# The first input projection of the second block: its second weight chunk is requested at the landing of another gather

## The reference

```
u_sel = u[ids]                                  # 128 rows of 1024 per token
h     = gelu(einsum('td,ted->te', x, u_sel))    # one dot product per pick
v_sel = v[ids]
out   = einsum('te,ted->td', gates * h, v_sel)  # weighted sum of 128 rows
x     = layer_norm(alpha * x + out)
```

## Time and profile before

| what | us |
|---|---|
| median of 3 runs | 2751.7 |
| lowest and highest | 2751.35, 2753.34 |
| span of the profiled execution | 2749.7 |
| TensorE busy in the span | 2495.3 |
| last gather used by VectorE (from the span's start) | 1558.26 |
| last mix of the expert stage ends | 1562.63 |
| chunk 1 and chunk 2 used up by TensorE | 1578.16 |

### The profile page before, as it was taken

The page is one execution under the profiler, slowest core; times in us unless marked ns, Lnnn a source line. Parts: engine busy times, 40 slices in busy tenths (PEclk is TensorE's granted clock), DMA queues, the critical chain, the costliest instruction groups (busy, mean ns, idle before and its releaser), DMA issues.

```text
span 2749.7 us, 29400 instructions
## 1 busy us (share of the span) xinstructions
PE 2495.3 (91%) x9829; PEld 1558.5 (57%) x9829; DVE 1761.0 (64%) x3952; ACT 995.1 (36%) x2016; POOL 652.1 (24%) x636
## 2 busy tenths in 40 slices
PE   8989888798987999877877899999999999999999
PEld 4544443364452565533323357885688668865787
DVE  2678876766758667678776566554666556546654
ACT  2136322234322354223222145432444444424443
POOL 0134344433434324334444220002000020002000
PEclk9999999999999999999999999999999999999999
DMA  7599999999999999999999833543254415523452
GB/s 294 210 379 420 414 421 404 421 421 421 407 420 421 420 394 411 420 422 419 421 419 418 347 123 138 184 167 153 70 206 153 170 46 199 185 117 123 153 190 100
DMA packets 112402, 798.99 MB, mean 291 GB/s; under 512 B 13076, under 2 KB 15719, under 8 KB 20247
## 3 DMA queue, kind: packets, MB, share of 16 engines
q0 software_dynamic: 74464, 540.07, 47.7%
q1 hardware_dynamic: 37814, 257.40, 24.7%
HBM read 796.36 MB, written 4.22 MB: 291 GB/s over the span
## 4 chain that ended last, share of the span: by engine, by line
PE 62%; DMA 20%; DVE 11%; issue 3%; ACT 3%; POOL 0%; SPq 0%; DVEq 0%; ACTq 0%; POOLq 0%
PE psum L1372 13%; PE psum L1480 13%; PE psum L1103 11%; DMA arena<-in_peer_uv,scratch 11%; DMA weights<-in_peer_uv,scratch 8%; PE psum L1437 8%; PE psum L1439 4%; DVE heads_arena L2302 3%; PE psum L1189 2%; PE psum L1197 2%; PE psum L1175 1%; PE psum L1080 1%; PE psum L1164 1%; PE psum L1151 1%; ACT scratch L1809 1%
## 5 line engine op out<-in xcount | busy, mean ns | idle before, releaser
L1372 PE MATMUL psum<-weights,scratch 128*128 128x512 f32 x1024 | 493.5, 631 | 93.1 <-ACT scratch L1809 93.1
L1372 PE MATMUL psum<-arena,scratch 128*128 128x512 f32 x1024 | 474.8, 609 | 85.9 <-ACT scratch L1809 85.3
L2664 DVE TENSOR_TENSOR piece<-weights,piece 128x2048 fp32r<-128x2048 f32 x128 | 292.1, 2292 | 180.7 <-ACT piece L1901 180.7
L2818 POOL DMA_INDIRECT weights<-in_peer_uv,scratch x256 | 287.4, 1123 | 489.2 <-PE psum L1372 434.0
L1372 PEld LDWEIGHTS psum<-weights,scratch 128*128 128x128 f32 x1024 | 198.5, 201 | 361.5 <-issue 216.1
L1372 PEld LDWEIGHTS psum<-arena,scratch 128*128 128x128 f32 x1024 | 190.0, 193 | 343.2 <-issue 196.8
L2818 POOL DMA_INDIRECT arena<-in_peer_uv,scratch x256 | 282.2, 1103 | 395.2 <-PE psum L1372 382.7
L1803 ACT ACTIVATE scratch<-scratch 128x2 f32<-128x2 f32 x255 | 51.9, 203 | 865.3 <-DVE heads_arena L2302 859.4
L1480 PE MATMUL psum<-piece,hidden 128*128 128x512 f32 x1536 | 358.9, 390 | 0.0
L1103 PE MATMUL psum<-weights,xT 128*128 128x512 f32 (+2 forms) x792 | 334.1, 575 | 18.4 <-DMA weights<-in_w_qkv_a 8.5
L1437 PE MATMUL psum<-split_x,piece 128*128 128x512 f32 x896 | 318.6, 398 | 0.0
(11 more groups left out here) (268 smaller groups left out, 2771.1 us busy)
## 6 DMA issues: line engine op xcount, KB each, us to landing
weights<-in_w_up SPq DMA_DIRECT2D x64, 1024.0 KB, 4.9
weights<-in_w_down SPq DMA_DIRECT2D x64, 1024.0 KB, 4.9
weights<-in_w_kv_b SPq DMA_DIRECT2D x16, 1024.0 KB
weights<-in_peer_w_q SPq DMA_DIRECT2D x10, 1024.0 KB
weights<-in_a_w_in SPq DMA_DIRECT2D x5, 2048.0 KB, 11.4
weights<-in_w_q_b SPq DMA_DIRECT2D x8, 1024.0 KB
weights<-in_a_w_out SPq DMA_DIRECT2D x4, 2048.0 KB, 7.8
weights<-in_w_qkv_a SPq DMA_DIRECT2D x3, 2048.0 KB, 16.5
```

The source lines that it names most:

```text
L1372: mm = pe.matmul(psum[g.bank][:, :], diagonal[:, n % DIAGONALS, :], row[:, D + half * BANK:D + (half + 1) * BANK], start=(k == 0), stop=(k ...
L2664: dve.tensor_tensor(split_piece[n][1][:, :], raw_piece[n], split_piece[n][0][:, :], ALU.subtract)\
L2818: pool.indirect_dma_start(gathered[n % GATHER_SLOTS], None, rows, bass.IndirectOffsetOnAxis(ap=expert[:, w % NT, k:k + 1], axis=0), elemen ...
```

## The change

SP's wait ahead of chunk 1 is for another gather: before, it was pick 511, the last; now it is pick 507, the fifth from the end (`SEAM_AFTER = 2 * 2 * 128 - 5`). The buffer is 507 % 8 = 3 in place of 7, and the count is the same, 16 * 64. Nothing else is changed: the same DMAs go out in the same order, with the same other waits.

```
+SEAM_AFTER = 2 * NT * SEL - 5
...
             for l in layers:
                 load_weights(l.inp, 0, 1)
                 if l.n == 0:
-                    last = WINDOWS * SEL - 1
-                    sp.wait_ge(gather_landed[last % GATHER_SLOTS], 16 * (last // GATHER_SLOTS + 1))
+                    sp.wait_ge(gather_landed[SEAM_AFTER % GATHER_SLOTS], 16 * (SEAM_AFTER // GATHER_SLOTS + 1))
                     load_seam_chunk(l.inp.chunks[1])
                 load_weights(l.inp, 2 if l.n == 0 else 1)
```

## The result

Six runs of the changed kernel have a median of 2760.35 us (2758.63 to 2764.2); six of the kernel before, beside them, 2751.84 (2748.85 to 2753.55). The ratio is 1.0029, with a 95% interval of 1.0019 to 1.0039: 8 us slower by the ratio, 8.5 by the medians. Eleven later runs of the same kernel gave 2760.06 against 2753.49, a ratio of 1.0024 (1.0014 to 1.0033).

What follows compares the result with a forecast made beforehand. The stage was taken as bound by gathers, paced by one late DMA engine. +6.8 - 1.27 + 1.5 = +7.0 us on 2749.7 gave 2756.7, plus 2.0 for the median: 2758.7 us; 8-in-10 range 2755.3 to 2762.2.

Steps and rivals of the forecast that it cites:

- What paces the stage: Mixes of picks at the seam: bound by gathers, 2.47 us per 1 MB, the slowest DMA engine setting pick 511's time.
- The free ride: Rival at the seam: late engine serves its gathers first, only TensorE's two waits vanish, 2750.4 us; chance 0.08.
- The requests: SP's queue: chunk 1 goes out near 1548.4, 9.9 us sooner, and chunk 2 near 1549.3 instead of 1559.1.
- The bill of the gathers: Slowest engine: 19 gather packets let 16 packets of chunk 1 and 3 of chunk 2 pass, pick 511 6.8 us late.
- What the projection gets: Projection behind the last mix: TensorE's waits of 0.97 and 0.30 us for chunks 1 and 2 go, -1.27 us.
- The tail: From the product of pick 511 to the end of its mix: unchanged at 4.37 us.
- The clock: TensorE before the last mix: an idle stretch lowers its clock, costing 0 to 2.9 us, taken as 1.5.
- The sum: Whole kernel: +6.8 - 1.27 + 1.5 = +7.0 us on the span of 2749.7.
- Smaller bill: Rival at the seam: chunk 2 passes too late, first packets need 5 us, or clock stays up; 2756.1 us; chance 0.14.
- Larger bill by blocks: Rival at the seam: weight packets pass in blocks, all 24 ahead of the last gather packet, +10.0, 2761.7 us; chance 0.12.

Runs made afterwards that it cites:

- bridged_fitted: The changed kernel plus 2, 1 and 4 idle TensorE matmuls ahead of the mixes of picks 508, 510 and 511; median +5.3 us against the kernel before.
- hold_second: The changed kernel, but chunk 2 waits for pick 511 again, so only chunk 1 is requested early; median +3.4 us against the kernel before.
- early_hold: The changed kernel with chunk 1 requested at pick 448, in mid-stage, and chunk 2 waiting for pick 511; median +1.5 us against the kernel before.
- changed_again: The changed kernel itself measured once more, nothing altered; 2760.06 us against 2753.49 for the kernel before, ratio 1.0024.
- bridged: The changed kernel plus 3, 2 and 7 idle TensorE matmuls ahead of the mixes of picks 508, 510 and 511; median +5.2 us against the kernel before.
- after_510: The changed kernel, but the wait is for pick 510, the last but one; median -2.2 us against the kernel before, -1.0 on a repeat.
- eighth: The changed kernel loading under 0.1 MB of chunks 1 and 2 instead of 4 MB, result not the reference's; median 0.0 us against the kernel before.
- small_4k: The changed kernel with chunk 1 sent as four DMAs of 512 KB, in 4 KB packets; median +0.9 us against the kernel before.
- whole_16k: The changed kernel with chunk 1 sent as one DMA of 2 MB, in 16 KB packets; median +9.4 us against the kernel before.

## Why the prediction was right

The forecast was 2758.7 us, 0.26% slower; measured were 2760.35, 0.29%, and 0.24% on the repeat. By its own steps:

- **What paces the stage.** Right: one engine, 6.25% of the DMA, sets the time of pick 511, and it has no idle time. The free ride, which the share of 0.06 in the earlier trace rows invites, did not happen.
- **The requests.** Chunk 1 went out as pick 507 landed and chunk 2 0.9 us behind it, as read from the earlier trace rows. That chunk 2 moves too is not in the diff; it is 2.5 of the 7.4 us.
- **The bill of the gathers.** 6.8 forecast, 7.43 measured (7.46 on the repeat). The step is right and the size short by one 16 KB packet: 16 x 0.31 + 4 x 0.61 = 7.4. The first weight packet came some 3.2 us after the request and not 3.5, so 20 gather packets were left and not 19. Bridged_fitted, with the same requests, had the forecast's 19, so this one packet is a draw too. For pick 510 the forecast had 10 packets and 3.2 us; by its own count, 19 less the 8 of the last gather, it is 11, and measured were 12, 3.76 us.
- **What the projection gets.** -1.27 forecast; the distance from the end of the last mix to the end of the second projection block shrank from 15.53 to 13.74 us, 1.8. The waits were all of the forecast; the other 0.5 is what TensorE loses at the start of a block behind a wait, which hides in the records' lengths: 16 + 16 records take 14.57 us with the wait between them, 32 in a row 13.90.
- **The tail.** Forecast as before, 4.37 us from the product of 511 to the end of its mix. With the clock up it is 4.13 (hold_second, 1567.53 + 1.98 - 1565.38): before the change the mix of 511 stood behind that of 510 on TensorE, and a late 511 doesn't. That is -0.2 us, which the forecast put at nothing.
- **The clock.** 1.5 forecast as the middle of 0 and 2.9. The mix of 511 took 3.37 us against 1.98 behind a wait at full clock, 1.4 us. The repeat shows 2.7 and the fitted bridge 0, so this term is a draw within those bounds, and part of the scatter of the changed kernel; that it fell next to the middle is luck. The forecast had one fall and there were two: the first stretched the mix of 508 and 509 to 5.40 us and cost nothing, because TensorE waited 3.98 us for pick 511 later on.
- **The sum.** 7.0 forecast; 7.4 - 1.8 - 0.2 + 1.4 = 6.8 in the profiled pair's seam, +8.1 in the repeat's. The mechanism held. The number is nearer than its terms, which is luck: the gathers came 0.6 us dearer, and the projection and the tail 0.8 us cheaper. The other 1.6 us of the profiled span (2758.1 - 2749.7 = 8.4) were there before the change begins.
- **The rivals.** Smaller bill: what hold_second built, and it got +3.4 us with the clock up. Larger bill by blocks: refuted by the steps of 4, 12 and 20 packets; its 9.8 us was reached only with 16 KB packets in turn.

## What to carry to other kernels

When a stage is bound by DMA, a load that is moved into its middle costs its full time: 2 MB cost 4.9 us at chunk 0 and 5.1 in early_hold. At the stage's end it costs what passes ahead of the last transfer, even when most engines are already idle, because that transfer lands with the slowest engine. The free headroom is only what the slowest engine still has to write before the first packet of the load: here one gather of 2.5 us, and requesting four ahead turned a gain of 1.8 us at the seam into a loss of 6.8 to 8.1. If a load has to run beside the last critical transfers, cut it into smaller contiguous runs: with chunk 1's at 16, 8 and 4 KB the cost to the gathers was 9.8, 7.4 and 3.3 us. This gains because only some 20 gather packets were left; what smaller runs do in the middle of the stage was not tried.

## What the runs showed of the hardware that was not expected

- The one-to-one alternation is so regular that the distance A repeated at 17.29, 17.32 and 17.32 us in three kernels that request alike (changed, changed_again, bridged). In the fourth, bridged_fitted, it was 0.6 us less: one packet of 0.61.
- One DMA engine can be 5 to 6 us (more than two gathers) behind the other fifteen in the last gathers, with a share of 6.7% where full use would be 100%. Why it is behind is open.
- Weight packets don't follow a request after a fixed time: on the late engine the first came 3.2 us after it with gathers queued, and at most 2.0 us after it once they had run out (after_510).
- A delay of 1.1 us in one gather can cost 3 us, when it lowers TensorE's clock (eighth). Waits of 1.92, 2.34 and 2.50 us were followed by a fall in small_4k, eighth and the changed kernel, and waits of 2.52 and 2.92 us were not in hold_second and whole_16k.
- An idle 128x512 float matmul counts as two records and took 0.88 us (bridged: 7 of them, 14 records, 6.17 us).
